# Hybrid decoder layer on one core: attention values made the stationary operand, two heads of both key heads per product, division moved ahead of the transposes

## The reference

```python
def swa_with_sinks(q, k, v, sinks):
    ...
    s_band = jnp.where(band_ok[None, :, None, None], s_band, MASK_VALUE)
    s_meta = jnp.where(meta_ok[None, :, None, None], s_meta, MASK_VALUE)
    sink = jnp.broadcast_to(sinks.astype(jnp.float32).reshape(1, 1, ATTN_KV_HEADS, G, 1, 1), s_meta.shape[:-1] + (1,))
    p = jax.nn.softmax(jnp.concatenate([s_meta, s_band, sink], axis=-1), axis=-1)
    p_meta = p[..., :N_META].astype(v.dtype)
    p_band = p[..., N_META:N_META + 2 * BLOCK].astype(v.dtype)
    o = (jnp.einsum('bnhgqk,bnkhd->bnqhgd', p_band, v_band)
         + jnp.einsum('bnhgqm,bmhd->bnqhgd', p_meta, v_meta))
    return o.reshape(B, T, ATTN_Q_W)
...
y_attn = swa_with_sinks(qa, ka, va, attn_sinks) @ w_attn_branch
```

## Time and profile before

| | us |
|---|---|
| median of 3 runs | 713.11 |
| lowest and highest | 712.53, 713.36 |
| the profiled execution's own time | 712.88 |
| its span in the profile | 711.0 |
| PE busy in that span | 682.6 |
| DVE busy | 377.9 |
| ACT busy | 207.2 |
| POOL busy | 103.2 |

### The profile page before, as it was taken

The page is one execution under the profiler, slowest core; times in us unless marked ns, Lnnn a source line. Parts: engine busy times, 40 slices in busy tenths (PEclk is TensorE's granted clock), DMA queues, the critical chain, the costliest instruction groups (busy, mean ns, idle before and its releaser), DMA issues.

```text
span 711.0 us, 11190 instructions
## 1 busy us (share of the span) xinstructions
PE 682.6 (96%) x4523; PEld 524.6 (74%) x4523; DVE 377.9 (53%) x673; ACT 207.2 (29%) x443; POOL 103.2 (15%) x131
## 2 busy tenths in 40 slices
PE   4999999999999999999989986999999999999998
PEld 2579999888788888888779985756656575756565
DVE  4547234687978778776683454261515252433514
ACT  5337132223433434341433342211120202020102
POOL 3400006887500000000000011110101010110000
PEclk9799999999999999999999995999999999999999
DMA  7431212301112111113336028798999999999953
GB/s 236 130 118 61 61 60 70 109 1 60 60 60 62 58 59 60 60 60 110 126 118 269 30 103 339 310 404 355 413 380 410 377 390 404 375 402 392 419 206 118
DMA packets 49797, 139.32 MB, mean 196 GB/s; under 512 B 6066, under 2 KB 28099, under 8 KB 41556
## 3 DMA queue, kind: packets, MB, share of 16 engines
q1 hardware_dynamic: 47298, 134.36, 50.0%
q0 software_dynamic: 2304, 4.20, 1.6%
q10 hardware_dynamic: 146, 0.07, 0.0%
HBM read 138.61 MB, written 4.19 MB: 201 GB/s over the span
## 4 chain that ended last, share of the span: by engine, by line
PE 87%; DVE 5%; ACT 3%; DMA 2%; issue 2%; POOL 1%; ACTq 0%; POOLq 0%; DVEq 0%
PE bank L873 16%; PE bank L556 13%; PE bank L557 12%; PE bank L558 12%; PE bank L886 8%; PE bank L981 7%; PE bank L783 2%; DVE y_lo L1673 1%; PE bank L838 1%; PE bank L756 1%; PE bank L782 1%; PE bank L845 1%; PE bank L781 1%; PE bank L716 1%; PE bank L720 1%
## 5 line engine op out<-in xcount | busy, mean ns | idle before, releaser
L1365 DVE TENSOR_TENSOR wlo<-wraw,whi 128x2048 fp32r<-128x2048 f32 (+1 forms) x26 | 58.7, 2260 | 30.8 <-ACT whi L1090 30.8
L556 PE MATMUL bank<-whi,xhi 128*128 128x256 f32 (+1 forms) x256 | 73.3, 286 | 0.0
L558 PE MATMUL bank<-whi,xlo 128*128 128x256 f32 (+1 forms) x256 | 71.8, 280 | 0.0
L557 PE MATMUL bank<-wlo,xhi 128*128 128x256 f32 (+1 forms) x256 | 71.7, 280 | 0.0
L556 PE MATMUL bank<-xhi,whi 128*128 128x512 f32 (+2 forms) x176 | 69.5, 399 | 1.6 <-DVE wlo L1365 1.6
L557 PE MATMUL bank<-xlo,whi 128*128 128x512 f32 (+2 forms) x176 | 68.3, 391 | 0.0
L558 PE MATMUL bank<-xhi,wlo 128*128 128x512 f32 (+2 forms) x176 | 67.6, 389 | 0.0
L873 PE MATMUL bank<-wgate,xgT 128*64 128x256 f32 x512 | 60.8, 392 | 1.0 <-DVE xgT L1641 1.0
L873 PE MATMUL bank<-wup,xgT 128*64 128x256 f32 x512 | 58.4, 381 | 0.0
L886 PE MATMUL bank<-wdown,hT 128*64 128x512 f32 x256 | 58.1, 595 | 0.0
L1090 ACT ACTIVATE whi<-wraw 128x2048 fp32r<-128x2048 f32 (+1 forms) x26 | 47.8, 1843 | 25.8 <-PE bank L558 18.7
(11 more groups left out here) (287 smaller groups left out, 1326.6 us busy)
## 6 DMA issues: line engine op xcount, KB each, us to landing
wgate<-in_expert_w_gate SPq DMA_DIRECT2D x32, 1024.0 KB, 8.4
wup<-in_expert_w_up SPq DMA_DIRECT2D x32, 1024.0 KB, 10.5
wdown<-in_expert_w_down SPq DMA_DIRECT2D x32, 1024.0 KB, 16.4
wraw<-in_w_in SPq DMA_DIRECT2D x17, 1024.0 KB, 5.6
wraw<-in_w_out SPq DMA_DIRECT2D x4, 1024.0 KB, 5.4
h<-in_x SPq DMA_DIRECT2D x4, 512.0 KB, 5.1
wraw<-in_w_gla_branch SPq DMA_DIRECT2D x2, 1024.0 KB, 5.1
wraw<-in_w_attn_branch SPq DMA_DIRECT2D x2, 1024.0 KB, 5.1
```

What stands on the lines that cost most here:

```text
L556: nc.tensor.matmul(ps, lhi(k), rhi(k), start=(k == 0), stop=False)
L557: nc.tensor.matmul(ps, lhi(k), rlo(k), start=False, stop=False)
L558: last = nc.tensor.matmul(ps, llo(k), rhi(k), start=False, stop=(k == kt - 1))
L1365: nc.vector.tensor_tensor(w_view(wlo[split_buffer(c)], c), w_view(wraw[c % 2], c), w_view(whi[split_buffer(c)], c).bitcast(F32), ALU.subtr ...
```

## The change

The product is turned round. The values (64 columns) become the stationary operand and the transposed probabilities stream, 256 columns at a time: two steps' heads of 128 tokens each. Key head j = 0 writes partitions 0 to 63 of the bank, j = 1 writes partitions 64 to 127, so the result already has features in its partitions. "PV" stands in every second step only, three steps behind its scores. oT has no transposes and no bank of its own: ACT and DVE split the product's bank directly. The rows of `w_attn_branch` are put in the order of those partitions on the host. Since tokens no longer lie in partitions there, the division moves ahead of the transposes: a new step "share" (DVE adds sum and sink term of two heads and takes the reciprocal; ACT multiplies the two heads' probabilities by it) stands between the unit and S, for the step before; the transposes now wait for it. "onorm" and `o_tok` are gone. Line numbers of the changed kernel are a little off those of the kernel before.

```diff
 
     def product(n):
         b, i = pairs[n]
-        return [("PV", b, i)] + ([("onorm", b)] if i == 3 else [])
+        return [("PV", b, i)] + ([("oT", b)] if i == 2 else [])
 
     for c in range(10, 18):
         s += [("prep", c + 1)]
         for u in range(2):
             n = 2 * (c - 10) + u
             b, i = pairs[n]
-            s += [("unit", c, u)] + (product(n - 2) if n >= 2 else [])
+            s += [("unit", c, u)] + (product(n - 3) if n >= 3 and n % 2 else [])
+            s += [("share",) + pairs[n - 1]] if n >= 1 else []
             s += [("S", b, i)] + ([("PT",) + pairs[n - 1]] if n >= 1 else [])
             if i == 2:
-                s += [("ogT", b)] + ([("oT", b - 1)] if b >= 1 else [])
+                s += [("ogT", b)]
             s += [("sig", c, u)]
-    s += [("prep", 19), ("unit", 18, 0)] + product(14) + [("PT",) + pairs[15], ("unit", 18, 1)] + product(15)
-    s += [("unit", 18, 2), ("oT", NB - 1), ("unit", 18, 3)]
+    s += [("prep", 19), ("unit", 18, 0), ("share",) + pairs[15], ("PT",) + pairs[15], ("unit", 18, 1)] + product(14)
+    s += [("unit", 18, 2), ("unit", 18, 3)]
     s += [("prep", 20)] + [("unit", 19, u) for u in range(4)]
...
-        ptm = [at(f"ptm{i}", 81 * K1 + 512 * i, [NM, P]) for i in range(2)]
-        pt = [at(f"pt{i}", place[0] + K1 * i, [P, 256]) for i in range(2)]
+        pt = [at(f"pt{i}", place[0] + 2 * K1 * i, [P, 2, 2 * P]) for i in range(2)]
-        o_tok = at("o_tok", place[0], [P, 512])
+        ptm = [at("ptm0", 81 * K1, [NM, 2 * P]), more("ptm1", [NM, 2 * P])]
...
-                                pe.wait_ge(*banks.emptied(("ogT" if name == "wg" else "oT", b)))
+                                pe.wait_ge(*banks.emptied(("ogT" if name == "wg" else "PV", b)))
...
                     _, b, i = step
                     if i == 0:
                         pv = banks.take(pe, "O", ("PV", b))
-                    for j in range(2):
-                        pe.wait_ge(*banks.emptied(("PT", b, i, j)))
-                        hd = j * 4 + i
-                        o = pv[:, hd * DH:(hd + 1) * DH]
-                        vc = slice(j * DH, (j + 1) * DH)
-                        if b > 0:
-                            nc.tensor.matmul(o, pt[j][:, 0:128], v_tok[:, b - 1, vc], start=True, stop=False)
-                        nc.tensor.matmul(o, pt[j][:, 128:256], v_tok[:, b, vc], start=(b == 0), stop=False)
-                        last = nc.tensor.matmul(o, ptm[j][:, :], vm[:, vc],
-                                                start=False, stop=True)
+                    for ii in (i, i + 1):
+                        for j in range(2):
+                            pe.wait_ge(*banks.emptied(("PT", b, ii, j)))
+                    heads = [(pv[j * DH:(j + 1) * DH, i * P:(i + 2) * P], slice(j * DH, (j + 1) * DH)) for j in range(2)]
+                    if b > 0:
+                        for j, (o, vc) in enumerate(heads):
+                            nc.tensor.matmul(o, v_tok[:, b - 1, vc], pt[j][:, 0, :], start=True, stop=False)
+                    for j, (o, vc) in enumerate(heads):
+                        nc.tensor.matmul(o, v_tok[:, b, vc], pt[j][:, 1, :], start=(b == 0), stop=False)
+                    for j, (o, vc) in enumerate(heads):
+                        last = nc.tensor.matmul(o, vm[:, vc], ptm[j][:, :], start=False, stop=True)
                     last.then_inc(s_pv, 1)
-                elif kind in ("oT", "ogT"):
+                elif kind == "ogT":
                     b = step[1]
-                    if kind == "oT":
-                        pe.wait_ge(*banks.emptied(("PV", b)))
-                    else:
-                        pe.wait_ge(s_ogn, b + 1)
-                    src = o_tok[:, :] if kind == "oT" else rgs[:, b, :]
+                    pe.wait_ge(s_ogn, b + 1)
                     ps = banks.take(pe, "unit", step)
                     for j in range(4):
-                        last = nc.tensor.transpose(ps[:, j * P:(j + 1) * P], src[:, j * P:(j + 1) * P], ident)
+                        last = nc.tensor.transpose(ps[:, j * P:(j + 1) * P], rgs[:, b, j * P:(j + 1) * P], ident)
...
                         st_ = att_stat[:, b % 2, :, hd:hd + 1]
                         p = prob[n % 4][:, 128 if b == 0 else 0:272]
                         nc.scalar.activation(p, p, ACT.Exp, bias=st_[:, 1, :], scale=SCALE,
-                                             accum_out=st_[:, 2, :]).then_inc(s_prob, 1)
+                                             accum_out=st_[:, 2, :]).then_inc(s_sum, 1)
                         nc.scalar.activation(st_[:, 3, :], sinks[:, hd:hd + 1], ACT.Exp,
                                              bias=st_[:, 1, :]).then_inc(s_es, 1)
+                elif kind == "share":
+                    _, b, i = step
+                    act.wait_ge(s_part, 4 * b + i + 1)
+                    for j in range(2):
+                        n = 2 * (4 * b + i) + j
+                        hd = j * 4 + i
+                        p = prob[n % 4][:, 128 if b == 0 else 0:272]
+                        nc.scalar.activation(p, p, ACT.Copy, scale=att_stat[:, b % 2, 4, hd:hd + 1]).then_inc(s_prob, 1)
                 elif kind == "PT":
                     _, b, i = step
                     name = ("PT", b, i, 0)
                     act.wait_ge(*banks.filled(name))
-                    if 4 * b + i:
-                        act.wait_ge(s_pv, 4 * b + i)
+                    if 4 * b + i >= 2:
+                        act.wait_ge(s_pv, (4 * b + i) // 2)
                     ps = banks.get(name)
-                    c0 = 128 if b == 0 else 0
-                    nc.scalar.activation(pt[0][:, c0:256], ps[:, c0:256], ACT.Copy)
-                    nc.scalar.activation(ptm[0][:, :], ps[0:NM, 256:384], ACT.Copy).then_inc(banks.read(name), 1)
+                    k0, tok = 1 if b == 0 else 0, slice(i % 2 * P, (i % 2 + 1) * P)
+                    keys = ps[:, k0 * P:2 * P].rearrange("p (k t) -> p k t", t=P)
+                    nc.scalar.activation(pt[0][:, k0:2, tok], keys, ACT.Copy)
+                    nc.scalar.activation(ptm[0][:, tok], ps[0:NM, 256:384], ACT.Copy).then_inc(banks.read(name), 1)
                 elif kind in ("oT", "ogT"):
                     b = step[1]
-                    act.wait_ge(*banks.filled(step))
+                    name = ("PV", b) if kind == "oT" else step
+                    act.wait_ge(*((s_pv, 2 * (b + 1)) if kind == "oT" else banks.filled(step)))
                     dst, s = (ohi, s_ohi) if kind == "oT" else (oghi, s_oghi)
-                    ps = banks.get(step)[:, :].rearrange("p (j t) -> p j t", j=4)
+                    ps = banks.get(name)[:, :].rearrange("p (j t) -> p j t", j=4)
                     nc.scalar.activation(dst[:, :, b * P:(b + 1) * P], ps, ACT.Copy).then_inc(s, 1)
...
                     _, b, i = step
                     name = ("PT", b, i, 1)
                     dve.wait_ge(*banks.filled(name))
-                    if 4 * b + i:
-                        dve.wait_ge(s_pv, 4 * b + i)
+                    if 4 * b + i >= 2:
+                        dve.wait_ge(s_pv, (4 * b + i) // 2)
                     ps = banks.get(name)
-                    c0 = 128 if b == 0 else 0
-                    nc.vector.tensor_copy(pt[1][:, c0:256], ps[:, c0:256])
-                    nc.vector.tensor_copy(ptm[1][:, :], ps[0:NM, 256:384]).then_inc(banks.read(name), 1)
-                elif kind == "onorm":
-                    b = step[1]
-                    st_ = att_stat[:, b % 2, :, :]
-                    dve.wait_ge(s_es, 8 * (b + 1))
-                    link(nc.vector.tensor_tensor(st_[:, 4, :], st_[:, 2, :], st_[:, 3, :], ALU.add))
-                    link(nc.vector.reciprocal(st_[:, 4, :], st_[:, 4, :]))
-                    dve.wait_ge(s_pv, 4 * (b + 1))
-                    if b:
-                        dve.wait_ge(*banks.filled(("oT", b - 1)))
-                    nc.vector.tensor_tensor(o_tok[:, :].rearrange("p (h d) -> p h d", d=DH),
-                                            banks.get(("PV", b))[:, :].rearrange("p (h d) -> p h d", d=DH),
-                                            st_[:, 4, :].unsqueeze(2).to_broadcast([P, HQ, DH]), ALU.mult)\
-                        .then_inc(banks.read(("PV", b)), 1)
+                    k0, tok = 1 if b == 0 else 0, slice(i % 2 * P, (i % 2 + 1) * P)
+                    keys = ps[:, k0 * P:2 * P].rearrange("p (k t) -> p k t", t=P)
+                    nc.vector.tensor_copy(pt[1][:, k0:2, tok], keys)
+                    nc.vector.tensor_copy(ptm[1][:, tok], ps[0:NM, 256:384]).then_inc(banks.read(name), 1)
+                elif kind == "share":
+                    _, b, i = step
+                    n = 4 * b + i
+                    sums, sink, both = (att_stat[:, b % 2, k, i:HQ:4] for k in (2, 3, 4))
+                    dve.wait_ge(s_es, 2 * (n + 1))
+                    link(nc.vector.tensor_tensor(both, sums, sink, ALU.add))
```

(11 more changed lines are left out.)

## The result

The change takes 721.09 us (median of 4 runs, 719.61 to 721.44) where the kernel before, run beside it, takes 712.82: ratio 1.0134, interval 1.0106 to 1.0162. Ratio and interval are an estimate over the single runs; the two medians by themselves have 1.0116. A second set, of six runs, gave 718.62 against 710.81, ratio 1.0106 (1.0082 to 1.0129). So the change is 8 us slower. The forecast was slower by 3.7 (716.8 us, range to 720.0): right in direction, less than half of the size, and 721.09 lies above the range.

A forecast was written before the change was run, and what follows sets the result against it. PE, busy without a gap, was taken to bound the attention stage. Waits of 19.2 us against 17.5 won give +1.7; with 2.0 for a clock fall, 713.1 becomes 716.8 us, range 711.8 to 720.0.

The forecast's parts named there:

- What goes from PE: Attention stage on PE: shorter products win 15.8 us, dropped oT transposes 1.7, together 17.5 us less work.
- the entry of the product: Switch into the two-column form at each of eight products: estimated 0.15 us each, between nothing and 0.3.
- a drain of 0.33 at every change: Tiling changes at both ends of eight products: 5.3 us instead of 1.2, about 4 later; chance 0.07 shared with Rival 4.
- Clock: PE's long wait at the stage end: one fall to half clock, 2.0 us, between nothing and 3.0.
- What is added, and who waits: Attention stage: PE waits for share ahead of the transposes, mainly in even and oT steps, 19.2 us including the end.
- The multiplication: ACT multiplying 128x272 probabilities by a column in share: taken as 0.40 us, ends 0.25 and 0.56.
- The end: Behind the last scores: share queues behind DVE's sigmoid, split and drain, so PE waits 5.65 us in one piece.
- (1): Rival for the attention stage: the clock does not fall, 714.8 us; chance 0.20.
- rival 2: PE's waits in the stage are shorter than worked out: 711.8 us, no measurable change; chance 0.13.
- Rival 3: Branch stage from 329 us absorbs PE's lateness, so the end wait costs nothing: 709.2 us, faster; chance 0.10.
- Rival 4: In the products the two key heads do not run side by side: 9.7 us more, 726.5; chance 0.07 shared with the drain.
- 17.5 won against 19.2 waited: Attention stage total: PE work removed against the sum of PE's waits, giving +1.7 us before the clock.

The follow-up runs named there:

- c0: The change unaltered, profiled a second time beside the filling runs: one clock fall in the middle, 18.0 us of waits, stage 196.87 us.
- c1: a1 with the end of the stage reordered (two branch units ahead of the last transposes, sigmoid and weight split behind them): 696.84 us.
- c2: The change with useless matmuls filling PE's waits ahead of the transposes: first scores to attention branch 153.24 us, the change 156.53 and 154.71.
- c4: The change with useless matmuls (21) filling only the wait at the end: second stretch 20.30 us, the change 21.85 and 21.72.
- a3: The change without share, nothing divided, so the new product alone: 700.53 us, stage -10.6 us against the kernel before.
- d2: The change with the product's passes ordered one key head after the other instead of alternating column halves: 732.57 us.
- d3: The change with oT moved from ahead of share to behind the copies of PT in the same step: 726.21 us.
- a1: The change with every share in the step of its own scores, ahead of the sigmoid: 703.95 us, 0.85% faster than the kernel before.
- b2: b1 with every share moved into the step of its own scores: 710.15 us against 710.09 for the kernel before.
- a2: The change with only the last pair's share moved ahead of the last sigmoid: ratio 1.0113 against the kernel before.
- b1: The kernel before with only the division moved ahead of the transposes, the product left token-major: 720.02 us.
- d1: c1 with the 16 rows of the meta tokens zero-padded to 128: 694.86 us, ratio 0.9782 against the kernel before.

## Why the prediction was right in direction and too small

Against the forecast of +3.7 the stage ledger of the two profiles of the change is:

```
                                                 three falls   one fall
forecast                                              +3.7       +3.7
products 1.59 and 1.16 instead of 1.5 and 1.05        +0.8       +0.8
14 units 5.73 instead of 5.64                         +1.3       +1.3
transposes behind a wait 0.72 instead of 0.63, x12    +1.1       +1.1
scores ahead of a wait 0.84 instead of 0.77, x11      +0.8       +0.8
waits 16.6 and 18.0 instead of 19.2                   -2.6       -1.2
falls in the middle, 1.57 each                        +4.7       +1.6
fall at the end 1.5 instead of 2.0                    -0.5       -0.5
third stretch 42.21 and 42.16 instead of 42.63        -0.4       -0.5
sum                                                   +8.9       +7.1
measured                                              +9.0       +7.2
```

- **What goes from PE: the term that failed in both executions.** "Together 17.5 us of PE work" was 4.0 too good (the first four lines behind the forecast). PE is busy 139.89 us in the first two stretches of the change and 136.66 in c0, instead of 147.08; with the 6.2 and 3.1 us that the falls add in the ledger taken off, 13.4 and 13.5 us of work are gone. In c1, without a wait behind the scores and without a fall, 15.1 are gone. With these 4.0 and every other term as forecast the time would be 720.8 us, outside the range already; with the falls in the middle alone (2.5 us net, below) it would not. The largest piece is the unit's end, 0.09 dearer in each step: 268.08 to 273.81, 5.73, where it was 277.03 to 282.67, 5.64. I had looked for a price at the entry of the product and took it eight times at 0.15; what I did not see is that a unit directly in front of scores pays it too (the change and c1 both have 5.73 to 5.76 in steps without a product). The trace of before had such a unit, the first of the stage, from 182.68 to 188.44, and it took 5.76:

```profile
182.68 0.51 PE L556 MATMUL bank<-xhi,whi 128*128 128x512 f32 x1
...
188.44 0.50 PE L754 MATMUL bank<-kT,qT 64*128 64x128 f32 x4
```

In the product, the pass of 16 rows has its 0.14, and the rest of 1.59 - 1.35 is not taken apart. The rule that I weighed (the Trainium skill, TensorEngine Tiling, Key Properties: changing the tiling mode drains the TensorE) has the right sign; a drain of 0.33 at every change is not what the runs show, with 0.09 and 0.14. The last two of the four lines belong to the waits: where PE waits, nothing overlaps the end of the scores, and the second head's transposes wait for the second multiplication.

- **Clock: the count that failed.** I wrote "I expect one fall of the clock there", at the long wait, because I compared only this wait with the 2.96 us in the earlier trace rows. The waits of 1.5 us I took to be harmless. With a unit of 7.08 instead of 5.73 and transposes of 0.94 instead of 0.72, a fall costs 1.57 us of PE work, and c2 shows that it goes when the wait is filled. But part comes back, since the next wait is then 0.33 instead of 1.05. So a fall in the middle is worth about 0.85 us net, 2.5 us where there are three.
- **What is added, and who waits**: the places and sizes hold. Forecast 0.5, 1.1, 1.2, then 1.5, 1.5, 1.1 in the even, the oT and the following step, 5.65 at the end; c0 measured 0.43, 1.03, 1.17, then 1.46, 1.48, 1.05 and 5.63. None in odd steps without oT, as said. The multiplication takes 0.94 for two, 0.486 each, where I took 0.40 and a range to 0.56. By one rule it could have been had: the Trainium skill (ScalarE: Activation LUTs, What ACT_TABLE_LOAD costs) gives a fixed part, a part per element and one more per pointer operand, by which 272 elements with a pointer for the scale take an estimated 0.51; the trace agrees, with 0.486. What I left out is the second multiplication, which the second head's transposes wait for.
- **The end** came as forecast: 5.63 us and a fall. c4 prices the fall at 1.4 to 1.6, within my nothing to 3.0. It is that cheap because half of its 6.8 us lies in the wait; under work the same 6.8 us cost 3.1 in a3.
- **Rivals.** The clock did fall (1). The waits were not shorter by what rival 2 needs. Rival 3 would have shown the branch starting late and ending on time: its third stretch is 42.21 instead of 42.63 us, so PE's lateness passes on. Rival 4 would have cost 12 us (d2).
- **The sum as a method**: I took 17.5 won against 19.2 waited; it was 13.4 won against 16.6 to 18.0 waited. And I called each wait a cost of its own. d3 shows that they are one quantity: DVE's chain from scores to scores, less what PE has to do meanwhile. Read that way the profile also says what to do, which a1, b2 and c1 then did.

Open: why the falls in the middle come three times in one execution and once in another (a2 and d2, with the same waits, had all three; c4 had one at another wait); and if the 2 us that c2 lost in the branch is a rule.

## What to carry to other kernels

Work taken off the engine that bounds a stage is only won in the steps where no other engine's chain is as long; take a step apart and compare the two chains in it before adding up removed work. An operation that something on the critical engine waits for belongs directly behind its own inputs in its engine's queue: the same 64 small operations cost 10 us behind a sigmoid and nothing ahead of it. When a gapless stage gets gaps, price the clock for each of them, not for the longest. And when a matmul's neighbour in the program gets another shape, look for both kinds of neighbour in the trace before calling the rest unchanged: 0.09 us, fourteen times, was not in the sum.

## What the runs showed of the hardware

- In a stage otherwise full, idle times of TensorE of 1.5 us (1.49 in the first profile of the change, 1.48 in c0, 1.55 and 1.57 in c4) were followed by 3.4 us at 1.2 GHz, in some executions and not in others; the waits of 1.46 one step earlier in the change were followed by none. Single waits of 0.84 (b1) and of 0.7 and less (c1) were not either; one of 2.0 us was, with 6.8 us (a3).
- 64-column matmuls into the two column halves ran side by side where the halves alternate in the program, and not where one follows the other: 1.59 against 3.16 us for the same twelve passes (d2).
- A pass of 16 rows instead of 128 cost a product 0.14 us (d1). A unit takes 5.73 ahead of the scores or of the new 64-column product, and took 5.64 ahead of the old product with its 128 stationary columns.
